# Sample rows of the last two experts added on chip by gate matrices, and sample state products from stacked key and value parts

## The reference

```
z = rmsnorm(x) @ w_in                      # a, b (convolution), q, k, v, g (retention, 4 heads of 128)
o, new_state = retention(q, k, v, state)   # new_state[b, h] = gamma_h^8 * state[b, h] + (k * zeta)^T v over b's 8 rows
x = x + concat(silu(layernorm(conv)), silu(g) * groupnorm(o)) @ w_out
t = rmsnorm(x)
x = x + sum over the 2 chosen of 32 experts: gate * (silu(t @ w_gate[e]) * (t @ w_up[e])) @ w_down[e]
ple = rmsnorm(p @ w_ple)
x = x + ple * sigmoid(x @ w_ple_gate)
y = rmsnorm(x)                             # outputs: y of both groups, new convolution and retention states
```

## Time and profile before

| | before |
|---|---|
| median of 3 runs | 711.6 us (710.62 to 712.16) |
| profiled execution | 710.11 us |
| its span, first to last instruction | 708.3 us |
| PE busy | 679.8 us (96%) |
| DVE busy | 564.3 us (80%) |
| ACT busy | 401.3 us (57%) |
| POOL busy | 273.2 us (39%) |
| mean granted TensorE clock | 0.992 |

### The profile page before, as it was taken

One profiled execution on the slowest core, in us unless ns is written; L12 is line 12 of the kernel. 1 busy time (PEld: TensorE's weight loads), 2 busy tenths in 40 slices (PEclk: granted clock), 3 DMA queues, 4 the chain that ended last, 5 costly groups with the idle time before them and its releaser, 6 DMA issues.

```text
span 708.3 us, 13342 instructions
## 1 busy us (share of the span) xinstructions
PE 679.8 (96%) x4892; PEld 623.1 (88%) x4892; DVE 564.3 (80%) x814; ACT 401.3 (57%) x539; POOL 273.2 (39%) x233
## 2 busy tenths in 40 slices
PE   7999999998999999979999999999999999998995
PEld 5999999998989889738999999999999999976884
DVE  4599999986782443658888998888898988968785
ACT  6431322334451222577888888888888988852222
POOL 1151497789346220023434444444444444210101
PEclk9999999999999999999999999999999999999998
DMA  9551421220057282716899899999999999675211
GB/s 293 187 149 38 142 93 60 83 97 12 1 171 235 82 260 91 284 38 219 321 343 351 333 353 352 353 358 364 392 369 381 369 370 365 234 289 190 75 60 59
DMA packets 51438, 156.14 MB, mean 220 GB/s; under 512 B 8842, under 2 KB 30538, under 8 KB 38331
## 3 DMA queue, kind: packets, MB, share of 16 engines
q1 hardware_dynamic: 35905, 133.97, 52.5%
q10 hardware_dynamic: 9346, 12.13, 5.2%
q0 software_dynamic: 6144, 9.45, 4.0%
HBM read 149.83 MB, written 17.59 MB: 236 GB/s over the span
## 4 chain that ended last, share of the span: by engine, by line
PE 74%; DVE 8%; POOL 5%; issue 5%; DMA 4%; ACT 2%; ACTq 0%; SPq 0%; POOLq 0%; DVEq 0%
PE bank L557 67%; PE bank L561 6%; DMA out<-front 1%; DMA ring<-in_w_in 1%; DVE front L1619 1%; POOL uext L2117 1%; DVE front L1620 1%; DMA uext<-expert_rows 1%; DVE z L1313 1%; DVE front L1646 1%; POOL z L2205 1%; POOL grs L2198 1%; POOL uext L2116 1%; ACT front L2027 1%; DVE z L1454 1%
## 5 line engine op out<-in xcount | busy, mean ns | idle before, releaser
L557 PE MATMUL bank<-ring_parts,hT_high 128*128 128x256 f32 (+1 forms) x1260 | 184.4, 289 | 0.1
L557 PEld LDWEIGHTS bank<-ring_parts,hT_high 128*128 128x128 f32 x1260 | 165.3, 189 | 4.1 <-DVE ring_parts L1219 0.3
L1342 DVE TENSOR_TENSOR ring_parts<-ring,catT_parts 128x2048 fp32r<-128x2048 f32 x64 | 146.0, 2281 | 1.0 <-ACT catT_parts L1874 1.0
L557 PE MATMUL bank<-catT_parts,hT_high 128*128 128x256 f32 (+1 forms) x1042 | 140.3, 285 | 1.7 <-issue 0.8
L557 PEld LDWEIGHTS bank<-catT_parts,hT_high 128*128 128x128 f32 x1042 | 128.9, 189 | 2.9 <-issue 1.0
L1874 ACT ACTIVATE catT_parts<-ring 128x2048 fp32r<-128x2048 f32 x64 | 123.6, 1931 | 5.4 <-PE bank L557 4.5
L1487 DVE TENSOR_TENSOR ring_parts<-ring,down_high 128x2048 fp32r<-128x2048 f32 x31 | 71.2, 2295 | 25.4 <-ACT down_high L1964 14.1
L1188 DVE SCALAR_TENSOR_TENSOR bank<-uext,cpar,bank 128x512 f32<-128x512 f32 x116 | 86.8, 749 | 0.0
L2261 POOL DMA_INDIRECT expert_rows<-front,cur_code x32 | 31.4, 983 | 130.7 <-issue 111.9
L2097 POOL TENSOR_TENSOR ring_parts<-ring,ring_parts 128x2048 fp32r<-128x2048 f32 x11 | 50.7, 4607 | 58.7 <-ACT ring_parts L1695 58.7
L557 PE MATMUL bank<-down_high,cv_parts 128*128 128x512 f32 x248 | 65.1, 404 | 0.0
(11 more groups left out here) (304 smaller groups left out, 1160.5 us busy)
## 6 DMA issues: line engine op xcount, KB each, us to landing
ring<-in_w_expert_gate SPq DMA_DIRECT2D x32, 1024.0 KB
ring<-in_w_expert_up SPq DMA_DIRECT2D x32, 1024.0 KB
ring<-in_w_expert_down SPq DMA_DIRECT2D x32, 1024.0 KB
ring<-in_w_in SPq DMA_DIRECT2D x12, 1024.0 KB
ring<-in_w_out SPq DMA_DIRECT2D x4, 1024.0 KB
ring<-in_w_ple_gate SPq DMA_DIRECT2D x4, 1024.0 KB
catT<-in_x_prompt SPq DMA_DIRECT2D x4, 512.0 KB, 5.2
z<-in_x_prompt SPq DMA_DIRECT2D x4, 512.0 KB, 6.8
```

Of the source, the lines that this page charges most:

```text
L557: return nc.tensor.matmul(out, lhsT, rhs, start=start, stop=stop, skip_group_check=True)
L1342: V.tensor_tensor(ring_r[:, 3 * par + m, :], ring[:, 3 * par + m, :], cat_r[:, m * CHUNK:(m + 1) * CHUNK].bitcast(F32), ALU.subtract).then ...
```

## The change

Two parts. **Sample states:** k (times decay) is split into a high part, stored twice (rows 0 to 63 and 64 to 127), and a low part; v is stored as its high part on rows 0 to 63 and its low part on rows 64 to 127, and masks are made over 128 rows. A product becomes two fp32r products (128 rows, and 64 rows with the low part of k). The results go to three banks in turn. The parts of k lie in `x2_lo`, hence in `qTs` and `qTx`, and SP's load of `ple_w` waits for all eight products. **Last two experts:** for sample tokens the rows of the last two experts are no longer read back from DRAM. DVE makes 0/1 matrices of their places (`late_places`), PE spreads their gates by a product with ones, DVE multiplies (`late_scaled`), and PE multiplies the matrices with `yout` in SBUF; the gates of these two experts are taken out of the kept gates (`late_gates`), with which the other rows, loaded before the last two scatters land, are added (`x2_kept`). The expert rows of the sample tile are first filled with rows of x, so that nothing undefined is read. Around this, the overflow work moves into the first loop, `pick_gates` and the new gate work stand after step 0 of the last loop and `ple_norm` with `late_places` after step 1, ACT makes gate chunk 0 before the last hidden copy and copies y after it, the last down product uses other banks, the gate chunks are taken in the order 0, 1, 3, 2, the transposes of the second tile stand behind the whole of `gate_first`, and the 74 idle products are gone.

```diff
-        vmask = [... for t in (flat_s[0:NS, 0:NB * HD], cv[0:NS, 5 * PLE:5 * PLE + NB * HD])]
+        vmask = [... for t in (sext_r[:, :], cv_r[:, 5 * PLE:5 * PLE + NB * HD])]
+        k_high, k_low, v_parts = flat_low[:, D:D + 512], flat_low[0:NS, D + 512:2 * D], front_r[:, 4 * D:4 * D + 512]
+        def state_bank(n):
+            return bank[(6, 4, 5)[n % 3]][:, :]
...
 # SP
+            for k in range(2):
+                sp.dma_start(moe2[SEQ:T, k, :], x_rows(TT - 1)).then_inc(S["p_in"], 16)
...
-            sp.wait_ge(S["o_done"], TT)
-            sp.wait_ge(S["p_in"], 16 * TT)
+            sp.wait_ge(S["kvs_done"], 2 * NH)
+            sp.wait_ge(S["p_in"], 16 * (TT + 2))
             sp.dma_start(ple_w[:, :], w_ple[0].rearrange("(p k) n -> p (k n)", k=2)).then_inc(S["p_in"], 16)
             sp.wait_ge(*used(12))
             load(0, ring[:, 0, :], gate_rows(0))
...
+                if s == 2:
+                    for par in range(2):
+                        sp.wait_ge(scattered[par], 8 * NE - 16)
+                    sp.dma_start(first_rows[0:r, :, :], moe2[at:at + r, :, :]).then_inc(moe_in[0], 16)
                 load(s, slot2(s), gate_weights(s))
+                if s == 0:
+                    down_in(NE // 2 - 1, 1)
...
 # PE
-                    if n >= 2:
-                        pe.wait_ge(S["rs_upd"], n - 1)
-                    mm(bank[(6, 4)[n % 2]][:, :], kz[0:NS, h * HD:(h + 1) * HD], vmask[h % 2][:, 4 * a:4 * a + 4, :],
-                       True, True).then_inc(S["kvs_done"], 1)
+                        pe.wait_ge(S["k_parts"], 3)
+                    if n >= 3:
+                        pe.wait_ge(S["rs_upd"], n - 2)
+                    out, v = state_bank(n), vmask[h % 2][:, 4 * a:4 * a + 4, :]
+                    mm(out, k_high[:, h * HD:(h + 1) * HD], v, True, False)
+                    mm(out, k_low[:, h * HD:(h + 1) * HD], v[0:NS], False, True).then_inc(S["kvs_done"], 1)
...
             for q in range(NX):
                 step(LOOPS - 1, q, last=q == NX - 1)
+                if q == 1:
+                    pe.wait_ge(S["picks_done"], 3)
+                    mm(bank[7][:, 0:2 * NS], C("ones", NS), diag, True, True).then_inc(S["rank_done"], 1)
             down_plain(LOOPS - 1, NX - 1)
+            pe.wait_ge(S["one_hot"], 3)
+            for a in range(2):
+                for par in range(2):
+                    pe.wait_ge(S["y_ready"], 2 * NE - 2 if par == 0 else 2 * NE - 1 + a)
+                    m = mm(bank[7 - 6 * a][0:NS, :], at_rows[:, par, :], yout[:, par, a * 512:(a + 1) * 512], par == 0, par == 1)
+                m.then_inc(S["rank_done"], 1)
...
-            idle_products(74, 3)
             x2_T(0)
...
                 if n == 0:
-                    gate_first(0)
+                    gate_first()
                     x2_T(1)
-                    gate_first(1)
                     continue
...
 # DVE
+            def late_gates():
+                g = gates[0:NS, TT - 1, :]
+                then(V.tensor_tensor(late_gate, late_one, bc(g, 1, 2), ALU.mult))
+                then(V.tensor_reduce(late_sum, late_gate, AX.X, ALU.add))
+                V.tensor_tensor(diag, bc(ident[0:NS, 0:NS], 1, 2), bc(late_sum, 2, NS), ALU.mult).then_inc(S["picks_done"], 1)
+                then(V.tensor_reduce(kept_gate, late_gate.rearrange("p e k -> p k e"), AX.X, ALU.add))
+                then(V.tensor_tensor(kept_gate, g, kept_gate, ALU.subtract))
+            def late_places():
+                then(V.tensor_copy(row_at, tokidx[:, NE - 2:NE]))
+                then(V.tensor_scalar(row_at, row_at, -1.0, float(SEQ), ALU.mult, ALU.add))
+                then(V.tensor_tensor(at_rows, bc(C("lane")[:, 0:NS], 1, 2), bc(row_at, 2, NS), ALU.is_equal))
+            def late_scaled():
+                dve.wait_ge(S["rank_done"], 2)
+                V.tensor_tensor(at_rows, at_rows, bank[7][:, 0:2 * NS]..., ALU.mult).then_inc(S["one_hot"], 1)
...
             for q in range(1, NX):
                 step(0, q)
+                if q == 1:
+                    overflow_ends()
+                if q == 2:
+                    overflow_info()
...
                 step(LOOPS - 1, q, last=q == NX - 1)
                 if q == 0:
+                    pick_gates()
+                    late_gates()
+                if q == 1:
                     ple_rstd()
                     ple_norm(TT - 1)
+                    late_places()
                 if q == 2:
-                    pick_gates()
-            overflow_info()
+                    late_scaled()
+            gate_low(0)
+            gate_low(1)
...
-            for c in range(3):
-                gate_low(c)
-            x2_first()
-            x2_out_first()
-            x2(1)
+            x2_kept()
+            for a in range(2):
+                x2_late(a)
+                x2_low_first(a)
             gate_low(3)
+            gate_low(2)
+            x2_second()
...
 # ACT
+            for at in (0, NS):
+                A.activation(k_high[at:at + NS, :], kz[0:NS, :], ACT.Copy).then_inc(S["k_parts"], 1)
...
+                if last:
+                    gate_high_part(0)
+                    hid_plain(i, q)
                 if not first:
                     y_copy(*before(i, q))
-                if last:
-                    hid_plain(i, q)
...
 # POOL: the scatters of the last two experts leave out the sample rows
-                scatter(LOOPS - 1, q, last=q == NX - 1)
+                scatter(LOOPS - 1, q, last=q == NX - 1, bound=2 * (T if q < 2 else SEQ) - 1)
```

More of the change, by code:

```diff
@@ L166, in build @@
         junk_rows = place("junk_rows", [P, D], F32)
+        first_rows = place("first_rows", [P, 2, D], F32)
         x2_lo = place("x2T_low_parts", [P, 2, KT, P])
@@ L874, in _ @@
             sample_states((2, 3))
-            pe.wait_ge(S["p_in"], 16 * TT)
+            pe.wait_ge(S["p_in"], 16 * (TT + 2))
             p_T((0, 1))
@@ L1039, in gate_part, with gate_first @@
                 return w.rearrange("p (k n) -> p k n", k=2)[:, k % 2, lo:hi]
-            def gate_first(half):
-                for k in range(4 * half, 4 * half + 4):
-                    if k == 0:
+            def gate_first():
+                for turn in range(KT):
+                    k = 2 * TURNS[turn // 2] + turn % 2
+                    if turn == 0:
                         pe.wait_ge(S["x2T_low"], 1)
                         pe.wait_ge(S["x2_low0"], 1)
-                    if k == 4:
+                    if turn == 4:
                         pe.wait_ge(S["x2T_high"], 1)
@@ L1442, in _ @@
             V.tensor_tensor(blockone, blockeq, bc(C("code"), 2, NBLK), ALU.mult).then_inc(S["one_hot"], 1)
+            then(V.tensor_tensor(late_one, bc(posb[0:NS, :, TT - 1], 1, 2), bc(C("expert", NS)[:, NE - 2:NE], 2, 2),
+                                 ALU.is_equal))
             dve.wait_ge(S["table_done"], 1)
@@ L1514, in pick_gates, with overflow_ends @@
                 then(V.tensor_tensor(gates[:, :, 1], gates[:, :, 0], e2, ALU.mult))
-            def overflow_info():
+            def overflow_ends():
                 jj = bc(C("ovj", 1), 2, NE)
@@ L1565, in x2, with x2_kept, x2_late @@
                                        ALU.add).then_inc(S["x2_done"], 2)
-            def x2_first():
+            def x2_kept():
                 i, r = ORDER[0], rows(ORDER[0])
-                for a, landed in ((0, S["first_in"]), (1, moe_in[0])):
+                dve.wait_ge(moe_in[0], 16)
+                for k in range(2):
+                    then(V.scalar_tensor_tensor(x1(i), first_rows[0:r, k, :], kept_gate[:, k:k + 1], x1(i), ALU.mult, ALU.add))
+            def x2_late(a):
+                dve.wait_ge(S["rank_done"], a + 3)
+                v = x1(ORDER[0], a)
+                V.tensor_tensor(v, bank[7 - 6 * a][0:NS, :], v, ALU.add).then_inc(S["x2_done"], 1)
@@ new lines, in x2_low_first, with x2_second @@
+            def x2_low_first(a):
+                high, low = gate_parts(0, a)
+                if a:
+                    dve.wait_ge(S["x2T_high"], 1)
+                else:
+                    dve.wait_ge(S["x2T_low"], 1)
+                    dve.wait_ge(S["rp_out"], 16)
+                V.tensor_tensor(low, quads(0, a), high.bitcast(F32), ALU.subtract).then_inc(S["hlo_sb" if a else "x2_low0"], 1)
+            def x2_second():
+                i = ORDER[1]
+                for a, landed in ((0, S["first_in"]), (1, moe_in[1])):
@@ L1586, in x2_out @@
+                    V.scalar_tensor_tensor(x1(i, a), yin2[:, 1, cols], gates[:, i, 1:2], x1(i, a), ALU.mult,
+                                           ALU.add).then_inc(S["x2_done"], 1)
             def x2_out(n):
@@ L1945, in y_copy @@
                         act.wait_ge(S["d_done"], NE + a)
-                    A.activation(yout[:, par, a * 512:(a + 1) * 512], bank[5 + a][:, :], ACT.Copy).then_inc(S["y_ready"], 1)
+                    A.activation(yout[:, par, a * 512:(a + 1) * 512], bank[(2 if last else 5) + a][:, :],
```

(16 more changed lines are left out.)

122 lines of the change are left out of this document (70 added, 52 removed).

## The result

| | before | changed |
|---|---|---|
| median | 711.88 us (4 runs, 710.62 to 712.55) | 719.28 us (4 runs, 718.32 to 720.89) |
| profiled execution, span | 710.11, 708.3 | 720.89, 719.1 |
| mean granted TensorE clock, profiled | 0.992 | 0.978 |

The ratio is 1.0115, 95% interval 1.0096 to 1.0135: the change made the kernel 7.4 us slower. I had said 715.5 (706.8 to 719.0): the right direction, half the size, 0.3 beyond the range. In the changed kernel products stand under L580 and transposes under L584.

What follows compares the result with a forecast made beforehand. The prediction took TensorE's queue, busy for 96% of the span, as the bound. Its terms 4.1 + 1.3 + 0.6 + 2.0 - 4.0 = +4.0 gave 714.1 us profiled, 715.6 for the median, stated as 715.5 (range 706.8 to 719.0).

Steps and rivals of the forecast that it cites:

- A: Sample state products on PE at 240 us: fp32r products 0.23 to 0.24 apart, p_T starting 3.2 us earlier.
- B: SP's later loads delay the sample states' store; PE waits 7.3 us for norm2(0), A's gain is lost: +4.1 us.
- The clock: Low TensorE clock brought by the 7.3 us wait for norm2(0): +1.3 us.
- C: DVE's added work in the expert loop makes PE late: +0.6 us in the first loop, +2.0 in the last.
- D: The end, after the last expert: gate product 5.0 us earlier, second tile 4.0 earlier, passed on by PE's tail: -4.0 us.
- (2): Rival: the store is late but DVE's additions in the loop are hidden: +1.4 us, 713.0; chance 0.16.
- Rival (1): The sample states' store is not held up by the loads: -4.6 us, 707.0; chance 0.17.
- (3): Rival: both Rival (1) and (2) hold: -7.2 us, 704.4; chance 0.05.
- Rival (4): The end gives nothing, because the kept rows or the late gates are late: +8.0 us, 719.6; chance 0.10.

Runs made afterwards that it cites:

- e2: The changed kernel with the four heads' state products in four forms (blocked or flat mask, second product of 64 or 128 rows): 719.62 us in one run.
- e8: e7 with the second state product of all 128 rows for all four heads: 707.88 us (9 runs), ratio to before 0.9959.
- e7: e1 with DVE's added work moved out of the steps in which PE waits for hidden: 709.64 us (12 runs), ratio to before 0.9975.
- e5: The kernel before, with only SP's load of ple_w made to wait for all eight state products: 721.44 us (4 runs), ratio to before 1.0138.
- e10: e8 with the 1 MB ple_w load issued just ahead of the sample states' store: 713.26 us (10 runs), ratio to before 1.0025.
- e1: The changed kernel with SP issuing expert 0's chunks first and ple_w only after the states' store has landed: 711.31 us (10 runs), ratio to before 1.0008.
- e6: The changed kernel with the whole state part taken back, the last two experts' part kept: 712.67 us (10 runs), ratio to before 1.0020.
- e9: e8 with the reordered end of e4: 709.11 us (12 runs), ratio to before 0.9967.
- e3: The changed kernel with 60 unread bf16 products on PE ahead of the first transposes of h2: 720.55 us (4 runs).
- e4: The changed kernel with the second tile's rows added and transposed before the last four gate products: 719.93 us (4 runs).
- e11: The changed kernel with 80 unread bf16 products on PE ahead of the first transposes of h2: 717.89 us (4 runs).

## Why the prediction was half right

**A, the products: mis-sized.** I priced a product at 0.23 from a row in which all products have 128 rows. The alternation of 128 and 64 rows made it 0.43 (e2). PE gained 1.1 at p_T, not 3.2. Even at 0.23 it would not have been 3.2, since PE then waits for DVE's evictions (e2): e8, with all rows full, gained 1.9 from the first state product to p_T (9.81 us for 11.75).

**B, the store: right in mechanism and duration.** I said the store is issued at 250.6, lands at 267.6 (17.0 us) and PE waits 7.3. It took 16.9, and PE waited 7.50. But the loads are released by the products, so each microsecond that these did not gain moved the loads, the store and h2: +5.9 at h2_T(0), not +4.1. The page that I weighed (the Trainium skill, DMA: Bandwidth & Descriptors, "Issuing engines are not separate DMA queues") gave the same side of the sum as the rows; the store's 9.9, 12.6 and 16.9 us with nothing, 1 MB and 3.1 MB of SP's loads issued in the two microseconds ahead of it agree with it.

**The clock: the step that failed most.** I took +1.3, with a bound of 1.7 if all of a 3.4 us stretch met work. The stretch at the wait was 10.2 us, of which 5.9 met work, and cost 2.6; another, at the first expert, cost 1.2. My row for it was a place where 3.4 us of low clock followed 3.8 us of a nearly empty PE; a wait twice as long had a stretch three times as long, and in e2, at 7.14 us of wait, twice as long. I had written "twice that if it falls twice" and not put it into the range. With 5.9 for B, 3.7 for the clock (2.6, 1.2 and the table's -0.1), 2.0 for C and -2.3 for D the sum is +9.3 where I had +4.0; the start-up's 1.5 makes the 10.8 of the profiled executions. The medians differ by 7.4, since the profiled execution of the changed kernel is the slowest of its four and that of before is below all of its runs.

**C, DVE in the loop: right.** 0.45 and 1.6 for 0.6 and 2.0; e7 took the last pass back to its old length. The rival that hides it (2) falls.

**D, the end: the gain is at another chain.** PE's second tile came 4.3 nearer, as I said (4.0), but I wrote "from there the tail is PE's". It is not: the output follows the second tile's cast through DVE, ACT and POOL, and that moved 1.6 nearer, 2.3 at the last store (of which 0.7 is a wait of 0.75 for ACT that is gone). I read the chain that ended last by its shares, in which PE leads over the whole span, and not over the last 50 us.

The errors of A, the clock and D all had the same sign, and the range did not allow for that. Rival (1), a store not held up, is refuted by e5 and e10, and (3) with it. Rival (4) gave 719.6, close to the result, but by another mechanism: neither the kept rows nor the late gates were late (DVE began the kept rows at 643.58 with no wait, and the late gates were ready for PE).

## What to carry to other kernels

When a buffer is laid over another, the wait that this adds stands in some engine's queue: ask what is behind it there, and which transfer then starts beside which. Price a wait of TensorE twice, once for its length and once for the low clock behind it, and a gain at the end by the chain that reaches the last store, not by the busiest engine. Take a product's price from a row whose neighbours have the same number of rows.

## What the runs showed of the hardware

**Low clock behind a wait.** PE's wait for `norm2(0)`, the whole low stretch at it, the part of that stretch in which PE was at work again, and the time from h2_T(0) to h2_T(1), which is 8.45 us of unchanged work at full clock:

| kernel | wait, us | low clock, us | of it at work, us | h2_T(0) to h2_T(1), us |
|---|---|---|---|---|
| before, e1, e6 to e9 | 0.3 to 0.6 | 0 | 0 | 8.44 to 8.47 |
| e3 (60 products, then a wait) | 2.2 | 3.4 | 3.4 | 10.0 |
| e10 | 3.24 | 6.8 | 5.9 | 11.1 |
| e4 | 5.80 | 6.8 | 4.6 | 10.5 |
| e2 | 7.14 | 6.8 | 3.9 | 10.2 |
| changed | 7.50 | 10.2 | 5.9 | 11.1 |
| e5 | 7.54 | 10.2 | 4.8 | 10.6 |
| e11 (80 products, no wait) | 0 | 0 | 0 | 8.47 |

What a stretch costs is set by the part of it that meets work: 0.44 to 0.46 us for each microsecond of that part in all six kernels, while neither the wait nor the whole stretch orders the costs (e10, with less than half the changed kernel's wait, loses as much). These runs don't tell what sets the length beyond the order of this table, nor when it begins (2.9 to 5.5 us ahead of the wait's end in e2, e5 and the changed kernel, 0.7 behind it in e3). Low stretches at 290 to 330 us, in a part with short waits and small products, came and went between kernels whose code there is the same (none in the profile before, 6.8 in e8, two of 6.8 in e1); over 26 runs of the kernel before the mean clock lies between 0.985 and 0.993. In the three groups of such runs the time falls as the clock rises (correlation -0.86, -0.53 and -0.77), so the clock goes with a good part of the 3.7 to 5.4 us by which the runs of a group differ. Nine runs of e8 and twelve of e9 did not tell apart two kernels whose medians are 1 us apart.

**Rows and weight loads.** fp32r products of 512 columns that alternate between 128 and 64 rows stand 0.43 apart, each weight load (0.18) behind the product before it; with 128 rows throughout they stand 0.23 apart and the loads are under the products (e2). Half of the wider product's rows being zero cost nothing against the full products of the earlier trace rows, also 0.23 to 0.24 apart.

The Trainium skill, TensorE: Matmul & The Clock Gate, "The mechanism", says that a weight load is pulled ahead of products in flight when its row group does not conflict with theirs or when it goes to the background weight buffer, and then, from traces, that it overlaps them only when the row group differs. The runs differ from the second sentence: loads of 128 rows ran under products of the same 128 rows (e2). The loads that did not overlap were those whose number of rows was not that of the product before them, 64 behind 128 and 128 behind 64.
